# The first projection of a decoder trunk, fed by single k-tiles instead of four-tile blocks

## The chip, the cores and the metric

The kernel runs on one core of a Trainium2 chip. The metric is the device time of one execution in microseconds (us). Before the change the median of three runs was 577.66 us, the lowest 577.63, the highest 577.92.

The engines carry short names. PE is TensorE's matmul, PEld its weight load, DVE is VectorE, ACT is ScalarE, POOL is GpSimd, and SP is SyncE, which here only issues DMAs.

## The reference

One layer on 256 tokens of width 2048, all float32:

```
h    = rmsnorm(x) * g                     # row scale r = rsqrt(mean(x^2) + eps)
proj = h @ w_in                           # 2048 x 8192: dq dk dv mq mk mv gate
d_out, m_out = diff_attention(...), moba_attention(...)   # 8 + 8 heads, causal, ALiBi
x    = x + (concat(d_out, m_out) * silu(gate)) @ w_out
x    = x + memory cross-attention (4 heads) over rmsnorm(mem)
out  = rmsnorm(x) * final_g
```

The change touches only the beginning of `h @ w_in` and the mean of x² that goes with it.

## The kernel before

Every float32 product is made of three matmuls on rounded parts: an operand a is split into a_hi (rounded) and a_lo = a − a_hi, and a @ w becomes a_hi @ w_hi + a_hi @ w_lo + a_lo @ w_hi. ACT makes the hi part of every weight slab, DVE the lo part, and PE multiplies.

The projection goes by 8 pairs of heads. A pair needs 16 halves. A half is two k-tiles (2 × 128 rows of w_in) by 512 columns. Halves 0 to 7 of a pair make q and k in PSUM banks 0 and 1, halves 8 to 15 make v and the gate in banks 2 and 3. For a half PE runs 12 matmuls (2 k-tiles × 2 token tiles × 3 products), in `half_group` (L557 to L575).

The weight slabs go round through three buffers: `w_raw` (8 halves deep, filled by SP's DMAs), `w_hi` and `w_lo` (4 halves deep). ACT's `split_hi` (L803) may run as far ahead as the four slots allow, since it waits only for the DMA and for the half that used the slot before. DVE's `split_lo` (L1119) follows it. So the two converters can have up to four halves ready before PE needs them. A semaphore counts each step: `half_loaded`, `hi_made`, `lo_made`, `half_done`.

The left operand of the first pair is x itself, not yet scaled by r. It has to be turned so that the model dimension lies on the partitions. PE does this with transposes against an identity matrix, in `transpose_block` (L583): a block is four k-tiles, 8 transposes, into two PSUM banks. ACT (`block_hi_bank`, L822) then multiplies by the gain and rounds to `aT_hi`, DVE (`block_lo_bank`, L1138) makes `aT_lo`. Block 0 is turned before the first matmul, and blocks 1, 2 and 3 after halves 0, 2 and 4. x comes in five DMAs. While PE has nothing to do at the start it multiplies the identity by itself (`keep_busy`, 5, 4 and 2 times).

Between the halves the engines do other things, at places that the program fixes by the number n of the half. ACT squares and sums all of x at n = 4 and n = 5 (L1019). DVE, at n = 6, right after the lo part of half 8, copies the other gains and works out r = 1/sqrt(mean) by an integer seed and Newton steps, a chain of small dependent instructions (L1322 to L1332). Only then comes the lo part of half 9. The queues are in order on every engine: an instruction that waits holds all that stand behind it.

After the 16 halves of pair 0 the other seven pairs and the later stages follow in the same way, all fed by the same three buffers. The change leaves them as they are.

Of the kernel before, what the change touches and what calls it, by code (L numbers as in the profile page):

```python
# [22 lines left out]
F32 = mybir.dt.float32  # L23
# [7 lines left out]
P = 128  # L31
# [49 lines left out]
BLOCKS = (("x", 0, 4), ("x", 1, 6), ("x", 2, 4), ("x", 3, 6))  # L81


# [11 lines left out]
X_PARTS = ((0, 256), (256, 512), (512, 1024), (1024, 1536), (1536, 2048))  # L95
WARM_UP = (5, 4, 2)
# [31 lines left out]
def program(nc, x, mem, norm_mix_g, w_in, lambda_q1, lambda_k1, lambda_q2, lambda_k2,  # L128
            subln_g, w_out, norm_mem_g, mem_norm_g, w_q_mem, w_kv_mem, w_o_mem, final_g, out):
    with ExitStack() as ctx:  # L130
# [102 lines left out]
        x_sq, at = columns(0, NT)  # L233
        x_ms, at = columns(at, NT)
# [52 lines left out]
        first_hi = sem("first_hi")  # L287
        first_lo = sem("first_lo")
# [7 lines left out]
        block_made = sem("block_made")  # L296
        block_hi = sem("block_hi")
        block_lo = sem("block_lo")
# [8 lines left out]
        x_ms_ready = sem("x_ms_ready")  # L307
# [114 lines left out]
        def _(sp):  # L422
# [48 lines left out]
            load_x(0)  # L471
            for n in range(PAIR_HALVES):
                load_pair_half(DIFF, 0, 0, n)
                if n in (0, 1, 3, 5):
                    load_x((n + 1) // 2 + 1)
# [80 lines left out]
        def _(pe):  # L556
            def half_group(half, slot, banks, hi, lo, k0, first, last):  # L557


                first_half = isinstance(half, int) and half == 0  # L560
                if first_half:
                    pe.wait_ge(first_lo, 1)
                else:
                    wait(pe, lo_made, half + 1)
                for k in range(GK // 2):
                    if first_half and k == 1:
                        pe.wait_ge(lo_made, 1)
# [15 lines left out]
            def transpose_block(b):  # L583

                source, n, bank = BLOCKS[b]
                rows_of = {"x": xs, "mem": mems, "x1": xs}[source]
                before = [c for c in range(b) if BLOCKS[c][2] == bank]
                if source == "x" and n > 0:
                    pe.wait_ge(x_loaded[n + 1], 16)
                if source == "mem":  # L590
                    pe.wait_ge(mem_loaded, 16)
                if source == "x1":
                    pe.wait_ge(x1_ready, NT * (n + 1))
                if before:
                    pe.wait_ge(block_lo, 2 * (before[-1] + 1))
                for i in range(2):
                    if source == "x" and n == 0:
                        pe.wait_ge(x_loaded[i], 16)
                    for k in range(2):
                        for t in range(NT):  # L600
                            col = n * COLS + (2 * i + k) * P
                            m = pe.transpose(ps[:, bank + i, (k * NT + t) * P:(k * NT + t + 1) * P],  # L602
                                             rows_of[:, t, col:col + P], ident[:, :])
                    m.then_inc(block_made, 1)
                    if source == "x" and n == 0:
                        keep_busy(WARM_UP[1 + i])
# [42 lines left out]
            def pair_window(j, kind, first=False):  # L649

                for n in range(PAIR_HALVES):
# [7 lines left out]
                    if first and n < PAIR_HALVES // 2:  # L659
                        pe.wait_ge(block_lo, n + 1)  # L660
                    half_group(PAIR_HALVES * j + n, n % SPLITS, (0, 1) if n < PAIR_HALVES // 2 else (2, 3),
                               aT_hi, aT_lo, within * (GK // 2), within == 0, within == 2 * NG - 1)
                    if first:
                        if n in (0, 2, 4):
                            transpose_block(1 + n // 2)
# [17 lines left out]
            transpose_block(0)  # L683
# [120 lines left out]
        def _(act):  # L804
            def split_hi(half, i, turn, tail=False):
# [9 lines left out]
                if isinstance(half, int) and half == 0:  # L815

                    act.activation(w_hi[:, 0, 0], raw[:, 0], ACT.Copy).then_inc(first_hi, 1)
                    act.activation(w_hi[:, 0, 1], raw[:, 1], ACT.Copy).then_inc(hi_made, 1)
                    return
                act.activation(w_hi[:, i % SPLITS], raw, ACT.Copy).then_inc(hi_made, 1)  # L820

            def block_hi_bank(b, i):  # L822

                source, n, bank = BLOCKS[b]
                first_gain = {"x": 0, "x1": KO, "mem": 2 * KO}[source]
                act.wait_ge(block_made, 2 * b + i + 1)
                for k in (2 * i, 2 * i + 1):
                    into = cT_hi[:, k] if source == "x1" else aT_hi[:, GK * n + k]
                    gain = first_gain + GK * n + k
                    m = act.activation(into, ps[:, bank + i, (k % 2) * SEQ:(k % 2 + 1) * SEQ], ACT.Identity,  # L830
                                       scale=gainsT[:, gain:gain + 1])
                m.then_inc(block_hi, 1)
# [170 lines left out]
            block_hi_bank(0, 0)  # L1003
            split_hi(0, 0, 0)
            block_hi_bank(0, 1)
            split_hi(1, 1, 0)
            block_hi_bank(1, 0)
            split_hi(2, 2, 0)
            block_hi_bank(1, 1)
            for n in range(PAIR_HALVES):  # L1010
                if n in (3, 4, 5, 6):
                    block_hi_bank((n + 1) // 2, (n + 1) % 2)
                if n > 0:
                    split_hi(n + 2, n + 2, 0)
                if n == 4:
                    for part_loaded in x_loaded:
                        act.wait_ge(part_loaded, 16)
                if n in (4, 5):
                    act.activation(junk_row, xs[:, n - 4, :], ACT.Square,  # L1019
                                   accum_out=x_sq[:, n - 4:n - 3]).then_inc(x_summed, 1)  # L1020
                    act.wait_ge(x_summed, n - 3)
# [97 lines left out]
        def _(dve):  # L1119
            def split_lo(half, i, tail=False):  # L1120
# [4 lines left out]
                if isinstance(half, int) and half == 0:  # L1125

                    dve.wait_ge(first_hi, 1)
                    dve.tensor_tensor(lo[:, 0], w_raw[:, 0, 0], hi[:, 0].bitcast(F32), ALU.subtract
                                      ).then_inc(first_lo, 1)
                    dve.wait_ge(hi_made, 1)  # L1130
                    dve.tensor_tensor(lo[:, 1], w_raw[:, 0, 1], hi[:, 1].bitcast(F32), ALU.subtract
                                      ).then_inc(lo_made, 1)
                    return
# [3 lines left out]
            def block_lo_bank(b, i):  # L1137
                source, n, bank = BLOCKS[b]  # L1138
                first_gain = {"x": 0, "x1": KO, "mem": 2 * KO}[source]
                dve.wait_ge(block_hi, 2 * b + i + 1)  # L1140
                for k in (2 * i, 2 * i + 1):
# [365 lines left out]
```

## Time and profile before

| | before |
|---|---|
| median of three runs | 577.66 us |
| the profiled execution | 577.68 us |
| its span, first to last instruction | 575.9 us |
| PE busy | 565.1 us, 98% of the span |
| DVE, ACT busy | 422.8 us, 405.3 us |
| mean granted TensorE clock | 0.995 of full speed |
| first matmul of the projection | 8.33 us after the span's start |
| first matmul of half 8 | 33.61 us |

The span leaves out 1.78 us of the profiled execution that lie around it. The busy share of PE counts a matmul from its start to its modelled end, and neighbours overlap, so the distance between the starts of two matmuls is the better measure of the pace.

### The profile page before, as it was taken

To read this page: it belongs to the slowest core of one execution; us is meant where nothing else is said; L and a number is where in the kernel's file an instruction comes from. 1 tells how busy PE (TensorE), PEld (TensorE's weight loads), DVE (VectorE), ACT (ScalarE), POOL (GpSimd) and SP (SyncE) were. 2 spreads that over 40 slices of the span, in tenths; PEclk is the share of its full clock that TensorE was granted. 3 is DMA by queue.
4 is the path that set the end of the run, shared out by engine and by line. 5 is a ranking of instruction groups with operands and counts; after the bars stand their busy time and mean duration, and the time that the engine had idled before them with its cause. 6 is when DMAs were issued, how large, how long until landed. Compare 5 with 4: busy or idle time off the path is not lost.

```text
span 575.9 us, 8620 instructions
## 1 busy us (share of the span) xinstructions
PE 565.1 (98%) x2666; PEld 471.2 (82%) x2666; DVE 422.8 (73%) x710; ACT 405.3 (70%) x643; POOL 1.9 (0%) x25
## 2 busy tenths in 40 slices
PE   8999999999999999999999999999999999999993
PEld 7788888888888888888888888888888888888883
DVE  4678769778886877866766767767577887865875
ACT  5776967967868768766775784784589786845623
POOL 1000000000000000000000000000000000000000
PEclk9999999999999999999999999999999999999998
DMA  8997769658676776885875974979699977984203
GB/s 277 328 277 254 212 164 254 183 187 232 189 232 195 196 223 188 220 244 160 247 223 143 277 197 158 236 207 318 206 248 277 249 227 220 237 225 142 103 1 146
DMA packets 147356, 122.40 MB, mean 213 GB/s; under 512 B 63057, under 2 KB 129154, under 8 KB 146818
## 3 DMA queue, kind: packets, MB, share of 16 engines
q1 hardware_dynamic: 147298, 122.08, 73.4%
q8 instruction: 12, 0.20, 0.1%
q14 instruction: 14, 0.11, 0.1%
q10 hardware_dynamic: 32, 0.01, 0.0%
HBM read 106.06 MB, written 2.10 MB: 188 GB/s over the span
## 4 chain that ended last, share of the span: by engine, by line
PE 97%; DMA 1%; DVE 0%; SPq 0%; ACT 0%; issue 0%; ACTq 0%; DVEq 0%
PE ps L571 29%; PE ps L572 29%; PE ps L573 29%; PE ps L638 2%; PE ps L789 1%; PE ps L785 1%; PE ps L784 1%; PE ps L620 1%; DMA xs<-in_x 1%; PE ps L758 1%; PE ps L738 1%; PE ps L602 1%; PE ps L623 0%; PE ps L747 0%; PE ps L626 0%; SPq L432 0%
## 5 line engine op out<-in xcount | busy, mean ns | idle before, releaser
L1135 DVE TENSOR_TENSOR w_lo<-w_raw,w_hi 128x1024 fp32r<-128x1024 f32 x187 | 227.6, 1223 | 109.0 <-ACT w_hi L820 106.6
L820 ACT ACTIVATE w_hi<-w_raw 128x1024 fp32r<-128x1024 f32 x187 | 197.0, 1057 | 86.6 <-PE ps L573 84.6
L571 PE MATMUL ps<-w_hi,aT 128*128 128x512 f32 x576 | 226.5, 393 | 0.1
L572 PE MATMUL ps<-w_lo,aT 128*128 128x512 f32 x576 | 224.3, 389 | 0.0
L573 PE MATMUL ps<-w_hi,aT 128*128 128x512 f32 x576 | 224.2, 389 | 0.0
L573 PEld LDWEIGHTS ps<-w_hi,aT 128*128 128x128 f32 x576 | 108.1, 188 | 22.8
L571 PEld LDWEIGHTS ps<-w_hi,aT 128*128 128x128 f32 x576 | 108.2, 188 | 22.6 <-issue 0.5
L572 PEld LDWEIGHTS ps<-w_lo,aT 128*128 128x128 f32 x576 | 108.2, 188 | 21.6
L571 PE MATMUL ps<-w_hi,yT_hi 128*128 128x512 f32 x144 | 56.2, 390 | 0.0
L573 PE MATMUL ps<-w_hi,yT_lo 128*128 128x512 f32 x144 | 56.0, 389 | 0.0
L572 PE MATMUL ps<-w_lo,yT_hi 128*128 128x512 f32 x144 | 56.0, 389 | 0.0
L573 PEld LDWEIGHTS ps<-w_hi,yT_lo 128*128 128x128 f32 x144 | 27.0, 188 | 5.7
L571 PEld LDWEIGHTS ps<-w_hi,yT_hi 128*128 128x128 f32 x144 | 27.0, 188 | 5.6
L572 PEld LDWEIGHTS ps<-w_lo,yT_hi 128*128 128x128 f32 x144 | 27.0, 188 | 5.5
L1191 DVE RECIPROCAL pool<-pool 128x128 f32<-128x128 f32 x32 | 30.5, 953 | 1.1
L920 ACT ACTIVATE mems<-ps 128x1024 uint16<-128x1024 uint16 x16 | 15.5, 1020 | 18.5 <-PE ps L573 18.5
L941 ACT ACTIVATE pool<-pool,small 128x256 f32<-128x256 f32 (+1 forms) x48 | 21.3, 444 | 7.1 <-DVE small L1226 7.1
L890 ACT ACTIVATE pool<-mems 128x1024 uint16<-128x1024 uint16 x16 | 21.8, 1362 | 2.5 <-DMA mems<-mems 2.5
L1218 DVE SCALAR_TENSOR_TENSOR pool<-ps,small,alibi 128x256 f32<-128x256 f32 (+2 forms) x32 | 15.0, 512 | 5.8 <-PE ps L626 5.8
L1106 ACT ACTIVATE pool<-xs 128x512 f32<-128x512 f32 (+1 forms) x9 | 5.3, 586 | 15.3 <-DVE xs L1451 15.3
L881 ACT ACTIVATE probT<-mems 128x768 uint16<-128x768 uint16 x16 | 16.0, 1079 | 0.0
L955 ACT ACTIVATE mems<-pool 128x768 uint16<-128x768 uint16 x16 | 13.3, 832 | 2.9 <-DVE pool L1243 2.9
(181 smaller groups left out, 507.1 us busy)
## 6 DMA issues: line engine op xcount, KB each, us to landing
w_raw<-in_w_in SPq DMA_DIRECT2D x256, 256.0 KB, 3.2
w_raw<-in_w_out SPq DMA_DIRECT2D x64, 256.0 KB, 3.9
w_raw<-in_w_kv_mem SPq DMA_DIRECT2D x32, 256.0 KB, 4.2
w_raw<-in_w_q_mem SPq DMA_DIRECT2D x16, 256.0 KB, 2.9
w_raw<-in_w_o_mem SPq DMA_DIRECT2D x16, 256.0 KB, 3.4
mems<-in_mem SPq DMA_DIRECT2D x1, 2048.0 KB, 10.2
xs<-in_x SPq DMA_DIRECT2D x3, 512.0 KB, 7.6
w_raw<-in_final_g SPq DMA_DIRECT2D x1, 1024.0 KB, 4.6
```

Source lines behind the costliest of these rows:

```text
L571: pe.matmul(acc, hi[:, k0 + k, tok], w_hi[:, slot, k], start=first and k == 0, stop=False)
L572: pe.matmul(acc, hi[:, k0 + k, tok], w_lo[:, slot, k], start=False, stop=False)
L573: m = pe.matmul(acc, lo[:, k0 + k, tok], w_hi[:, slot, k], start=False, stop=last and k == GK // 2 - 1)
L820: act.activation(w_hi[:, i % SPLITS], raw, ACT.Copy).then_inc(hi_made, 1)
L881: act.activation(probT[:, u].rearrange("p i q -> p (i q)").bitcast(U16) .rearrange("p (c h) -> p h c", h=2), probT_planes[:, u].rearrange( ...
L890: act.activation(qkT_sb[:, :, t * P:(t + 1) * P].bitcast(U16) .rearrange("p i (q h) -> p h i q", h=2), qkT_planes[:, t].rearrange("p (h i ...
L920: act.activation(qk_planes[:, t].rearrange("p (h c) -> p h c", h=2), ps[:, t, :].bitcast(U16).rearrange("p (c h) -> p h c", h=2), ACT.Copy ...
L941: m = act.activation(prob_sb[:, u, c, cols], prob_sb[:, u, c, cols], ACT.Exp, bias=neg_max[:, u, t, c:c + 1], accum_out=exp_sum[:, c, u, t ...
L955: act.activation(prob_planes[:, u].rearrange("p (h c) -> p h c", h=2), prob_sb[:, u, 0, :].bitcast(U16).rearrange("p (c h) -> p h c", h=2) ...
L1135: dve.tensor_tensor(lo, w_raw[:, i % RAW], hi.bitcast(F32), ALU.subtract).then_inc(lo_made, 1)
L1191: dve.reciprocal(s, s).then_inc(silu_steps, 1)
L1218: dve.scalar_tensor_tensor(prob_sb[:, u, 0:kind.maps, cols], banks[:, :, cols], r[:, t:t + 1], bias, ALU.mult, ALU.add).then_inc(logits_re ...
```

## The change

In the first eight halves of pair 0 everything now goes by single k-tiles.

- **Transposes.** `transpose_rows(k)` turns one k-tile (2 transposes) into bank 4 + k mod 4. K-tiles 0 and 1 are turned before the first matmul, and k-tile k + 2 right after the matmuls of k-tile k.
- **Matmuls.** `first_half_group` runs one k-tile at a time: 2 matmuls hi × hi, then a wait for the lo parts, then 4 matmuls. The number of matmuls is the same.
- **ACT and DVE.** They make `aT` and `w` of one k-tile after the other: 128×256 of aT, then 128×512 of w, 16 times. Halves 8 and 9 are converted after k-tile 15, as before in the program's order, but now nothing of them can be done before.
- **Sums of squares.** ACT sums x in four pieces of 128×1024, one at the end of each of its halves 4 to 7. DVE adds the pieces up with one more instruction at the head of the chain for r.
- **Loads.** x comes in seven DMAs instead of five. Each of the first eight halves comes in three DMAs instead of two: one for its first k-tile, two for its second.
- **Warm-up.** The identity products are 3 and 4 instead of 5, 4 and 2.

The diff, cut to its core:

```diff
-BLOCKS = (("x", 0, 4), ("x", 1, 6), ("x", 2, 4), ("x", 3, 6))
...
-X_PARTS = ((0, 256), (256, 512), (512, 1024), (1024, 1536), (1536, 2048))
-WARM_UP = (5, 4, 2)
+X_PARTS = ((0, 128), (128, 256), (256, 512), (512, 768), (768, 1024), (1024, 1536), (1536, 2048))
+X_PART_BEFORE = (0, 2, 3, 4, 5, None, 6, None)
+X_PART_OF = (0, 1, 2, 2, 3, 3, 4, 4, 5, 5, 5, 5, 6, 6, 6, 6)
+WARM_UP = (3, 4)
...
+            def load_first_half(n):
+
+                if X_PART_BEFORE[n] is not None:
+                    load_x(X_PART_BEFORE[n])
+                sp.dma_start(w_raw[:, n, 0, :].rearrange("p (s c) -> p s c", c=2 * P),
+                             in_slabs[n][:, 0, 0:2, 0:2 * P]).then_inc(k_loaded[n], 16)
+                if n == 0:
+                    load_x(1)
+                for part, slab in enumerate(SLABS["diff", 0]):
+                    sp.dma_start(w_raw[:, n, 1, part * 2 * P:(part + 1) * 2 * P], in_slabs[n][:, 1, slab, 0:2 * P]
+                                 ).then_inc(half_loaded[n], 16)
...
+            def transpose_rows(k):
+
+                pe.wait_ge(x_loaded[X_PART_OF[k]], 16)
+                wait(pe, rows_lo, k - 3)
+                for t in range(NT):
+                    m = pe.transpose(ps[:, 4 + k % 4, t * P:(t + 1) * P], xs[:, t, k * P:(k + 1) * P], ident[:, :])
+                m.then_inc(rows_made, 1)
+
+            def first_half_group(n):
...
+                for i in range(GK // 2):
+                    k = 2 * n + i
+                    first, last = k == 0, k == KO - 1
+                    pe.wait_ge(rows_hi, k + 1)
+                    pe.wait_ge((k_hi, hi_made)[i], n + 1)
+                    for t in range(NT):
+                        pe.matmul(ps[:, t, :], aT_hi[:, k, t * P:(t + 1) * P], w_hi[:, slot, i],
+                                  start=first, stop=False)
+                    pe.wait_ge(rows_lo, k + 1)
+                    pe.wait_ge((k_lo, lo_made)[i], n + 1)
+                    for t in range(NT):
+                        pe.matmul(ps[:, t, :], aT_hi[:, k, t * P:(t + 1) * P], w_lo[:, slot, i],
+                                  start=False, stop=False)
+                        m = pe.matmul(ps[:, t, :], aT_lo[:, k, t * P:(t + 1) * P], w_hi[:, slot, i],
+                                      start=False, stop=last)
+                    if i == 1:
+                        m.then_inc(half_done, 1)
+                    if k + 2 < KO:
+                        transpose_rows(k + 2)
...
             pe.transpose(ps[:, 3, 0:KO], mix_gain[:, :], ident[0:KO, 0:KO]).then_inc(gainsT_made, 1)
-            transpose_block(0)
+            transpose_rows(0)
+            keep_busy(WARM_UP[1])
+            transpose_rows(1)
...
+            def first_split_hi(n):
+
+                for i in range(GK // 2):
+                    k = 2 * n + i
+                    act.wait_ge(rows_made, k + 1)
+                    act.activation(aT_hi[:, k], ps[:, 4 + k % 4, 0:SEQ], ACT.Identity, scale=gainsT[:, k:k + 1]
+                                   ).then_inc(rows_hi, 1)
...
+                    act.activation(w_hi[:, n % SPLITS, i], w_raw[:, n, i], ACT.Copy).then_inc((k_hi, hi_made)[i], 1)
...
+            for n in range(2 * NG):
+                first_split_hi(n)
+                if n >= 4:
+                    sum_squares(n % 2, (n - 4) // 2)
+            for n in range(2 * NG - 2, PAIR_HALVES):
+                split_hi(n + 2, n + 2, 0)
...
+            def first_split_lo(n):
+
+                for i in range(GK // 2):
+                    k = 2 * n + i
+                    dve.wait_ge(rows_hi, k + 1)
+                    dve.scalar_tensor_tensor(aT_lo[:, k], ps[:, 4 + k % 4, 0:SEQ], gainsT[:, k:k + 1],
+                                             aT_hi[:, k].bitcast(F32), ALU.mult, ALU.subtract).then_inc(rows_lo, 1)
+                    dve.wait_ge((k_hi, hi_made)[i], n + 1)
+                    dve.tensor_tensor(w_lo[:, n % SPLITS, i], w_raw[:, n, i], w_hi[:, n % SPLITS, i].bitcast(F32),
+                                      ALU.subtract).then_inc((k_lo, lo_made)[i], 1)
...
+                    dve.tensor_reduce(x_sq, x_sq2, axis=AX.X, op=ALU.add).then_inc(x_total, 1)
```

PE, the end of the start-up and the first half, in the kernel before. L602 are transposes of x, L571 to L573 the three products:

```order
L602 MATMUL ps<-ident,xs 128x128 x4
L580 UNCONDITIONAL_BRANCH
L581 MATMUL ps<-ident 128x128
L580 REGISTER_ALU
L580 COMPARE_AND_BRANCH
L571 MATMUL ps<-w_hi,aT 128x512
L572 MATMUL ps<-w_lo,aT 128x512
L573 MATMUL ps<-w_hi,aT 128x512
```

PE at the same place in the changed kernel. L595 are the transposes of x, L608 is hi × hi, L613 and L615 are the two products with a lo part:

```order
L595 MATMUL ps<-ident,xs 128x128 x2
L608 MATMUL ps<-w_hi,aT 128x512 x2
L613 MATMUL ps<-w_lo,aT 128x512
L615 MATMUL ps<-w_hi,aT 128x512
L613 MATMUL ps<-w_lo,aT 128x512
L615 MATMUL ps<-w_hi,aT 128x512
L595 MATMUL ps<-ident,xs 128x128 x2
L608 MATMUL ps<-w_hi,aT 128x512 x2
```

A pair of transposes now stands behind every six matmuls, 14 times, where a block of eight stood three times.

ACT from the w_hi of half 6 to that of half 9, in the kernel before (L820 makes w_hi, L830 makes aT_hi, L1019 sums squares):

```order
L820 ACTIVATE w_hi<-w_raw 128x1024
L1019 ACTIVATE pool,small<-xs 128x2048
L830 ACTIVATE aT<-ps,gainsT 128x256 x2
L820 ACTIVATE w_hi<-w_raw 128x1024
L1019 ACTIVATE pool,small<-xs 128x2048
L830 ACTIVATE aT<-ps,gainsT 128x256 x2
L820 ACTIVATE w_hi<-w_raw 128x1024 x3
```

ACT in the changed kernel, from k-tile 12 (half 6) to the halves 8 to 10. L837 makes aT_hi, L844 makes w_hi of one k-tile, L1021 sums squares, L830 makes w_hi of a whole half:

```order
L837 ACTIVATE aT<-ps,gainsT 128x256
L844 ACTIVATE w_hi<-w_raw 128x512
L837 ACTIVATE aT<-ps,gainsT 128x256
L844 ACTIVATE w_hi<-w_raw 128x512
L1021 ACTIVATE pool,small<-xs 128x1024
L837 ACTIVATE aT<-ps,gainsT 128x256
L844 ACTIVATE w_hi<-w_raw 128x512
L837 ACTIVATE aT<-ps,gainsT 128x256
L844 ACTIVATE w_hi<-w_raw 128x512
L1021 ACTIVATE pool,small<-xs 128x1024
L830 ACTIVATE w_hi<-w_raw 128x1024 x3
```

Before, the w_hi of half 8 is the second of the last three; after, it is the first, and the last aT_hi and a sum of squares stand right in front of it.

## Rows read from the trace of the kernel before

**Rows 1.** The page: busy time by engine, and the chain that ended last.

```profile
PE 565.1 (98%) x2666; PEld 471.2 (82%) x2666; DVE 422.8 (73%) x710; ACT 405.3 (70%) x643; POOL 1.9 (0%) x25
PE 97%; DMA 1%; DVE 0%; SPq 0%; ACT 0%; issue 0%; ACTq 0%; DVEq 0%
```

**Rows 2.** Timeline of PE, start-up: start, duration, engine, line, operation, idle time before.

```profile
1.73 2.51 PE L581 MATMUL ps<-ident 128*128 128x128 f32 x10 [1.73 <-POOL ident L542]
...
4.39 1.11 PE L602 MATMUL ps<-ident,xs 128*128 128x128 f32 x4
5.30 1.91 PE L581 MATMUL ps<-ident 128*128 128x128 f32 x8
7.46 0.66 PE L602 MATMUL ps<-ident,xs 128*128 128x128 f32 x4 [0.24 <-DMA xs<-in_x]
...
8.33 0.47 PE L571 MATMUL ps<-w_hi,aT 128*128 128x512 f32 x1
```

**Rows 3.** Timeline of PE after half 9: a pair of transposes between matmuls.

```profile
38.82 0.39 PE L573 MATMUL ps<-w_hi,aT 128*128 128x512 f32 x1
39.05 0.38 PE L673 MATMUL ps<-ident,pool 128*128 128x128 f32 x2
39.19 0.48 PE L571 MATMUL ps<-w_hi,aT 128*128 128x512 f32 x1
39.50 0.39 PE L572 MATMUL ps<-w_lo,aT 128*128 128x512 f32 x1
```

**Rows 4.** Timeline of PE: a block of eight transposes, and the step to half 2.

```profile
10.91 0.39 PE L573 MATMUL ps<-w_hi,aT 128*128 128x512 f32 x1
11.14 1.03 PE L602 MATMUL ps<-ident,xs 128*128 128x128 f32 x8
...
12.25 0.40 PE L572 MATMUL ps<-w_lo,aT 128*128 128x512 f32 x1
...
14.52 0.39 PE L573 MATMUL ps<-w_hi,aT 128*128 128x512 f32 x1
14.97 0.47 PE L571 MATMUL ps<-w_hi,aT 128*128 128x512 f32 x1
```

**Rows 5.** Timeline of PE: the last matmul of half 6, the first of halves 7 and 8.

```profile
30.66 0.39 PE L573 MATMUL ps<-w_hi,aT 128*128 128x512 f32 x1
30.89 0.39 PE L571 MATMUL ps<-w_hi,aT 128*128 128x512 f32 x1
...
33.61 0.39 PE L571 MATMUL ps<-w_hi,aT 128*128 128x512 f32 x1
```

**Rows 6.** Timeline of ACT.

```profile
6.76 0.63 ACT L817 ACTIVATE w_hi<-w_raw 128x512 fp32r<-128x512 f32 x1 [0.32 <-DMA w_raw<-in_w_in]
7.30 0.61 ACT L818 ACTIVATE w_hi<-w_raw 128x512 fp32r<-128x512 f32 x1
...
11.78 0.84 ACT L830 ACTIVATE aT<-ps,gainsT 128x256 fp32r<-128x256 f32 x2 [1.83 <-PE ps L602]
12.51 1.06 ACT L820 ACTIVATE w_hi<-w_raw 128x1024 fp32r<-128x1024 f32 x1
...
21.77 1.93 ACT L1019 ACTIVATE pool<-xs 128x2048 f32<-128x2048 f32 x1
23.57 0.21 ACT L1019 ACTIVATION_READ_ACCUMULATOR pool<-xs 128x1 f32 x1
```

**Rows 7.** Timeline of DVE.

```profile
7.42 0.69 DVE L1128 TENSOR_TENSOR w_lo<-w_raw,w_hi 128x512 fp32r<-128x512 f32 x1
...
13.60 1.23 DVE L1135 TENSOR_TENSOR w_lo<-w_raw,w_hi 128x1024 fp32r<-128x1024 f32 x1
...
31.52 0.19 DVE L1322 COPY gainsT<-ps 128x33 f32<-128x33 f32 x1
...
34.39 3.56 DVE L1135 TENSOR_TENSOR w_lo<-w_raw,w_hi 128x1024 fp32r<-128x1024 f32 x3
```

**Rows 8.** Busy time by stage, start-up left out; last columns: granted clock, DMA share, GB/s.

```profile
8.30:33.60 25.30, 25.24 (x124) 20.59 (x123) 17.63 (x35) 18.88 (x28) 0.00 (x0) 1.00 1.02 335
```

More of the change, by code:

```diff
@@ L233, in program @@
         x_sq, at = columns(0, NT)
+        x_sq2, at = columns(at, NT, 2)
         x_ms, at = columns(at, NT)
@@ L286, in program @@
         half_loaded = [sem(f"half_loaded{s}") for s in range(RAW)]
-        first_hi = sem("first_hi")
-        first_lo = sem("first_lo")
+        k_loaded = [sem(f"k_loaded{n}") for n in range(2 * NG)]
+        k_hi = sem("k_hi")
+        k_lo = sem("k_lo")
         hi_made = sem("hi_made")
@@ L306, in program @@
         x_summed = sem("x_summed")
-        x_ms_ready = sem("x_ms_ready")
+        x_total = sem("x_total")
         r_x_steps = sem("r_x_steps")
@@ L557, in half_group @@
             def half_group(half, slot, banks, hi, lo, k0, first, last):
[L560 to L564, printed above, removed]
+                wait(pe, lo_made, half + 1)
                 for k in range(GK // 2):
-                    if first_half and k == 1:
-                        pe.wait_ge(lo_made, 1)
                     for t in range(NT):
@@ L581, in keep_busy @@
                     pe.matmul(ps[:, 2, 0:P], ident[:, :], ident[:, :], start=True, stop=True)
[L583 to L606, printed above, removed]
@@ L814, in split_hi @@
                 wait(act, half_done, half - behind + 1)
[L815 to L819, printed above, removed]
                 act.activation(w_hi[:, i % SPLITS], raw, ACT.Copy).then_inc(hi_made, 1)
[L822 to L832, printed above, removed]
+            def first_split_hi(n):
[4 more added lines that the diff above has]
+                                   ).then_inc(rows_hi, 1)
+                    if i == 0:
+                        act.wait_ge(k_loaded[n], 16)
+                        wait(act, half_done, n - SPLITS + 1)
+                    else:
+                        act.wait_ge(half_loaded[n], 32)
+                    act.activation(w_hi[:, n % SPLITS, i], w_raw[:, n, i], ACT.Copy).then_inc((k_hi, hi_made)[i], 1)
             def split_turn(b, t):
@@ L1002, in _, with sum_squares @@
             act.wait_ge(gainsT_ready, 1)
[L1003 to L1021, printed above, removed]
+            def sum_squares(t, part):
+                loaded = range(5) if part == 0 else range(5, len(X_PARTS))
+                for n in loaded:
+                    act.wait_ge(x_loaded[n], 16)
+                cols = slice(part * DM // 2, (part + 1) * DM // 2)
+                act.activation(junk_row[:, 0:DM // 2], xs[:, t, cols], ACT.Square,
+                               accum_out=x_sq2[:, t, part:part + 1]).then_inc(x_summed, 1)
+                act.wait_ge(x_summed, 2 * part + t + 1)
+            for n in range(2 * NG):
[4 more added lines that the diff above has]
+                split_hi(n + 2, n + 2, 0)
                 if n == 10:
@@ L1124, in split_lo @@
                 lo = wo_lo[:, i - WO_HALF0] if over_yT else w_lo[:, i % SPLITS]
[L1125 to L1133, printed above, removed]
                 dve.wait_ge(hi_made, half + 1)
                 dve.tensor_tensor(lo, w_raw[:, i % RAW], hi.bitcast(F32), ALU.subtract).then_inc(lo_made, 1)
[L1137 to L1141, printed above, removed]
-                    hi, lo = (cT_hi[:, k], cT_lo[:, k]) if source == "x1" else \
-                             (aT_hi[:, GK * n + k], aT_lo[:, GK * n + k])
-                    gain = first_gain + GK * n + k
-                    m = dve.scalar_tensor_tensor(lo, ps[:, bank + i, (k % 2) * SEQ:(k % 2 + 1) * SEQ],
-                                                 gainsT[:, gain:gain + 1], hi.bitcast(F32),
-                                                 ALU.mult, ALU.subtract)
-                m.then_inc(block_lo, 1)
+            def first_split_lo(n):
[7 more added lines that the diff above has]
+                                      ALU.subtract).then_inc((k_lo, lo_made)[i], 1)
             def merge_turn(b):
@@ L1307, in _ @@
             dve.wait_ge(gainsT_ready, 1)
[L1308 to L1319 removed]
+            for n in range(2 * NG):
+                first_split_lo(n)
+            for n in range(2 * NG - 2, PAIR_HALVES):
+                split_lo(n + 2, n + 2)
                 if n == 6:
```

39 lines of the change are left out of this document (14 added, 25 removed).

## The prediction, made before the changed kernel was run

> **What bounds the kernel now.** I read the page first. PE is busy for 98% of the span and the chain that ended last is PE for 97% [rows 1]: the kernel is one long stream of matmuls, and no other engine holds it for long. The stages, in the view by windows, say the same for the stretch that the change touches. From 8.30 to 33.60 us PE is busy for 25.24 of 25.30 us at the full granted clock, while ACT and DVE are busy for 18.88 and 17.63 us [rows 8]. So a microsecond saved or lost in PE's stream before half 9 should stand unchanged in the end time, and I only have to find by how much the stream moves at that point. I take half 9 as the mark because what lies behind it is the same in both kernels. In the kernel before, half 8 starts at 33.61 [rows 5], and half 9 12 matmuls later. The pace is 2.72 us per half (30.89 to 33.61, rows 5), or 0.227 us per matmul. That puts half 9 at 36.33.
>
> Then I read the timelines of PE, ACT and DVE up to 40 us, since the change is about who is ahead of whom.
>
> **The start.** Now PE turns four tiles at 4.39, spins on the identity from 5.30, turns four more at 7.46 when the second part of x has landed, and starts the projection at 8.33 [rows 2]. The early operations are slow: eight identity records take 1.91 us, some 0.21 us from one to the next, and the transposes from 4.39 to 5.30 are 0.23 us apart. After the change two transposes instead of four stand at 4.39, so the identity products begin 0.46 us earlier, at 4.84; eight records of 0.21 end their slots at 6.55; two transposes follow, and the first matmul can start at about 7.05. Is its data there? ACT's first aT_hi can start at 5.15 (two transposes, the last ending near 5.08, and the 0.07 us from a transpose's end to ACT worked out below) and w_hi of k-tile 0 at 5.52, to end at 6.15. Its DMA is the second in the queue, 384 KB behind the start. In the kernel before 256 KB had landed by 4.39 [rows 2] and 768 KB by 6.76, where ACT waited for it [rows 6]; in proportion 384 KB land near 5.0. w_lo of k-tile 0 takes 0.69 us on DVE [rows 7] and ends near 6.9. So the first matmul stands at 7.05, **1.28 us earlier**. The bounds: 6.3 if the early operations run at the later pace, 7.5 if x's second part again comes when it came before. I take 7.05, from the rows at the pace that this stretch shows. The shorter first warm-up (3 for 5) falls into the wait for the gains' DMA, so I cost it at nothing. It could cost something only through the clock, a rival below.
>
> **PE's own stream.** The matmuls are the same 96. A block of eight transposes costs, from 10.91 to 12.25, 1.34 us less two paces of 0.227, that is 0.886 [rows 4]. The trace also has a lone pair of transposes, at 39.05: from 38.82 to 39.50 are 0.68 us less 0.454, so 0.226 [rows 3]. Three blocks (2.66) go and 14 pairs (3.16) come: **+0.50**. The bounds for a pair are 0.20 (a quarter of a block is 0.22) and 0.33, if the slow first matmul behind a pair were not shared as it is here. The 0.22 us that PE loses before half 2 (14.52 to 14.97, less 0.227, rows 4), where it waits for DVE's lo part that ends at 14.83 [rows 7], goes too: **−0.22**. If PE waited for nothing, half 8 would start at 33.61 − 1.28 + 0.50 − 0.22 = 32.61 and the kernel would gain 1.0 us.
>
> Waits come far more often: 48 instructions of PE's now carry one in this stretch, some 36 more than before. The step into half 7, which waits for two semaphores long met, takes 30.66 to 30.89, the plain pace [rows 5]: a wait already met costs nothing, and I cost them so. The Trainium skill (Advanced Engine Details and Errata, Miscellaneous Facts) gives 50 to 100 ns for reading a semaphore's value from a sequencer. If each of the 36 waits cost that in PE's stream, it would be an estimated 1.8 to 3.6 us more. The trace disagrees for a wait of this kind.
>
> **Where PE will wait.** K-tile k + 2 is turned after the matmuls of k, so ACT and DVE have the matmuls of k + 1 (1.59 us with its pair) to make both of its operands, and can never be further ahead. From the start of k-tile k: six matmuls 1.36; second transpose 0.10 later, 0.27 long; and ACT starts 0.07 after it (in the block at 11.14 the fourth transpose ends near 11.71 and ACT starts at 11.78, rows 4, 6). That is 1.80. One aT_hi takes ACT 0.365 to the next instruction (11.78 to 12.51 for two), w_hi of a k-tile 0.54 (6.76 to 7.30) and ends after 0.62 [rows 6]; w_lo begins 0.03 later and takes 0.69 [rows 7]; PE needs 0.14 more (14.83 to 14.97). The lo parts are ready at 1.80 + 0.365 + 0.62 + 0.03 + 0.69 + 0.14 = 3.64. PE wants them at 2 × 1.587 + 0.454 = 3.63. It just fits, with no reserve; I charge nothing.
>
> Four times ACT has a sum of squares behind its second k-tile. The trace only has the whole row: 1.80 us to the next instruction and 0.21 for the read [rows 6]. Half of it I take as 0.95 + 0.23 = **1.18** (w_hi of the same 1024 columns shows 0.95 from one to the next); the bounds are 1.0 and the whole 2.0. After the sum in half 4 ACT starts aT_hi of k-tile 10 at 0.905 + 1.18 = 2.09 after that of k-tile 9, and 1.59 would be in time: PE waits **0.50**. That delay is then slack for the next sum, and the gains' transpose after half 5 is slack for the third; I put 0.15 there.
>
> Now halves 8 and 9. In the kernel before DVE's chain for r starts at 31.52 and the lo part of half 9 at 34.39 [rows 7], so half 8 was ready at 31.6, two microseconds early, and half 9 at 34.39 + 1.23 = 35.62, 0.7 early. That lead is what the change takes away. After it:
> - half 8 without further waits at 32.61 + 0.50 = 33.11; k-tile 13 starts 4.31 before (1.587 + 2 × 1.36), at 28.80, and aT_hi of k-tile 15 at 28.80 + 1.80 = 30.60
> - ACT: + 0.905 (aT_hi, w_hi) + 1.18 (last sum) + 1.06 (w_hi of half 8) = 33.74
> - DVE: lo part of half 8, 33.77 + 1.23 = 35.00. PE should have started half 8 at 33.26 and stands for some 2.2 us, till the gain that follows the lo part is written too
> - DVE goes on at 34.91 with its chain, 34.39 − 31.52 = 2.87 us, then the lo part of half 9, 37.78 + 1.23 = 39.01; PE starts half 9 at 39.15, after another wait of 1.0
>
> Half 9 moves from 36.33 to 39.15: **+2.82 us**. The one more instruction in the chain (0.16 or so) is within the rounding. Behind this DVE converts a half in 1.2 us against PE's 2.72, so the lead comes back and PE waits no more; the transposes of q and k that SP sends off behind the lo part of half 9 move with it. Added to the profiled execution's own 577.68 us, which stands 0.02 above the median, this gives **580.5 us**.
>
> **Rivals.**
> A. *PE's clock rises later.* Rows 2 show slow transposes at 4.39 and quick ones at 7.46 (0.66 for four). If the shorter warm-up lets the rise slip behind the first matmuls, these run at twice the distance, 0.227 us more for each. Eight of them cost 1.8 us: 582.3. Against it: PE has nothing to do from about 3.3 to 4.17 only.
> B. *The loads come late.* SP issues ten DMAs more, about 0.5 us each; k-tile 14 would be sent off near 21 instead of 16 us. ACT wants it at 29. The queue moves 335 GB/s with its share at 1.02 [rows 8], and 6.1 MB need 18 us of that. If the smaller pieces cost a quarter of that rate, the last halves land some 1.3 us late: 581.8. The Trainium skill (DMA: Bandwidth & Descriptors, Anatomy of one DMA) gives each DMA about 2 us fixed, and half efficiency at some 860 KB. Pieces of 256 KB one behind the other would then reach an estimated 100 GB/s; the trace shows 335, so the fixed part overlaps here.
> C. *No stop at halves 8 and 9*, the not-slower side. If ACT and DVE are ahead after all, PE's stream alone decides and the end comes 1.0 us earlier: 576.7, within what can't be told from no change. For that the lo part of half 9 must be ready by 35.3, 3.7 us sooner than worked out. For it speaks that ACT and DVE have a quarter of this stretch free [rows 8]; against it that this free time lies before the transposes on which they wait.
> D. *As C, with the start at the early bound*: 0.75 less, 575.9, faster.
>
> **The numbers.** 0.2% of this kernel is 1.16 us, about what a measurement of it can tell from no change. My forecast holds with 0.64, with its own range 579.3 to 581.7: −1.2 for a sum or chain partly hidden and the start at its early bound, +1.2 for dearer pairs and a dearer sum. A has 0.10, B 0.07, C 0.12, D 0.05; 0.02 is for PE waits that cost by themselves. The range, 577.8 to 582.7, leaves out C and D and the ends of A. Faster by over 0.2% has 0.05, within 0.2% has 0.13, slower has 0.82.
>
> **What would show it.** In the changed kernel's profile: the first matmul near 7.05; k-tiles 1.59 us apart, with short waits for DVE's w_lo; a wait of half a microsecond at k-tile 10; PE idle for about 2 us before half 8 on DVE and for 1 us before half 9; and no idle time that was not there before after that. I am wrong if half 9 starts before 38 us, if PE waits at the k-tiles all along, or if the first matmuls are 0.4 us apart.

## The result

| | before | after |
|---|---|---|
| median | 577.80 us (5 runs, 577.63 to 578.33) | 580.67 us (5 runs, 580.43 to 580.96) |
| ratio, 95% interval | | 1.0049 [1.0038, 1.0060] |
| span of the profiled execution | 575.9 us | 578.6 us |
| first matmul of the projection | 8.33 us | 6.02 us |
| first matmul of half 8, of half 9 | 33.61, 36.33 us | 35.03, 38.93 us |

The changed kernel is 2.9 us slower. The forecast was 580.5, with the range 577.8 to 582.7. In later visits to the chip one execution of the kernel before (of 31) and one of `e4_three_ahead` (of 10) took some 1480 us; why is not known, and the intervals leave both out.

Here are PE's waits in the profile of the changed kernel (engine, line, whom it waited for: us in total, times, longest):

```profile
PE ps L588 <- POOL ident L555: 1.7, 1, 1.7
PE ps L578 <- DVE small L1314: 1.7, 1, 1.7
PE ps L578 <- DVE w_lo L1135: 0.9, 1, 0.9
```

The first was there before. The other two are new and stand before half 8 and half 9. L1314 is the small gain that DVE writes right behind the lo part of half 8, and PE waits for it too before it starts that half. The timeline of PE around them:

```profile
32.94 0.40 PE L615 MATMUL ps<-w_hi,aT 128*128 128x512 f32 x1
35.03 0.49 PE L578 MATMUL ps<-w_hi,aT 128*128 128x512 f32 x1 [1.69 <-DVE small L1314]
...
37.67 0.39 PE L580 MATMUL ps<-w_hi,aT 128*128 128x512 f32 x1
38.93 0.50 PE L578 MATMUL ps<-w_hi,aT 128*128 128x512 f32 x1 [0.87 <-DVE w_lo L1135]
```

At the plain pace of 0.227 us half 8 would start at 33.17 and half 9 2.72 us after half 8, at 37.75. So PE loses 1.86 and 1.18 us; the idle time in brackets is shorter, since it counts from the modelled end of the matmul before. ACT and DVE show what PE waits for:

```profile
30.31 0.47 ACT L837 ACTIVATE aT<-ps,gainsT 128x256 fp32r<-128x256 f32 x1 [0.53 <-PE ps L595]
30.68 0.62 ACT L844 ACTIVATE w_hi<-w_raw 128x512 fp32r<-128x512 f32 x1
31.20 1.05 ACT L1021 ACTIVATE pool<-xs 128x1024 f32<-128x1024 f32 x1
32.15 0.19 ACT L1021 ACTIVATION_READ_ACCUMULATOR pool<-xs 128x1 f32 x1
32.37 2.95 ACT L830 ACTIVATE w_hi<-w_raw 128x1024 fp32r<-128x1024 f32 x3
```

```profile
33.46 1.23 DVE L1135 TENSOR_TENSOR w_lo<-w_raw,w_hi 128x1024 fp32r<-128x1024 f32 x1 [1.44 <-ACT w_hi L830]
34.60 0.18 DVE L1312 COPY gainsT<-ps 128x33 f32<-128x33 f32 x1
...
37.66 3.49 DVE L1135 TENSOR_TENSOR w_lo<-w_raw,w_hi 128x1024 fp32r<-128x1024 f32 x3
```

The chain for r started at 31.52 before and the lo part of half 9 at 34.39 [rows 7]; they start at 34.60 and 37.66 now. From the start of half 9 to the end of the span it is 539.6 us before and 539.7 after: in the profiles all of the difference, 2.6 to 2.7 us, arises ahead of half 9. (The profiled execution of the changed kernel, 580.43 us, is the fastest of its five; the medians are 2.9 apart.)

### The profile page after: what moved, and what is told of

Read it like the earlier page. It is cut to its first block, busy times and chain, and to the rows that moved or that the text cites. A ratio compares the mean times of both kernels' runs of the same rounds, so it can differ in the third digit from the quotient of the medians.

```text
span 578.6 us, 8663 instructions
## 1 busy us (share of the span) xinstructions
PE 565.6 (98%) x2658; PEld 468.9 (81%) x2658; DVE 425.0 (73%) x718; ACT 407.0 (70%) x654; POOL 1.9 (0%) x25
## 4 chain that ended last, share of the span: by engine, by line
PE 97%; DVE 1%; ACT 1%; issue 0%; POOL 0%; ACTq 0%; POOLq 0%; DVEq 0%
PE ps L578 28%; PE ps L579 27%; PE ps L580 27%; PE ps L652 2%; PE ps L799 1%; PE ps L804 1%; PE ps L800 1%; PE ps L608 1%; PE ps L613 1%; PE ps L634 1%; PE ps L615 1%; PE ps L595 1%; PE ps L773 1%; PE ps L753 1%; PE ps L588 1%; DVE w_lo L1135 0%
## 5 line engine op out<-in xcount | busy, mean ns | idle before, releaser
L1135 DVE TENSOR_TENSOR w_lo<-w_raw,w_hi 128x1024 fp32r<-128x1024 f32 x180 | 218.9, 1222 | 107.6 <-ACT w_hi L830 105.7
L830 ACT ACTIVATE w_hi<-w_raw 128x1024 fp32r<-128x1024 f32 x180 | 189.5, 1057 | 84.7 <-PE ps L580 83.7
L578 PE MATMUL ps<-w_hi,aT 128*128 128x512 f32 x544 | 213.7, 393 | 2.6 <-DVE small L1314 1.7
L579 PE MATMUL ps<-w_lo,aT 128*128 128x512 f32 x544 | 211.9, 390 | 0.0
L580 PE MATMUL ps<-w_hi,aT 128*128 128x512 f32 x544 | 211.7, 389 | 0.0
L578 PEld LDWEIGHTS ps<-w_hi,aT 128*128 128x128 f32 x544 | 102.1, 188 | 24.4 <-DVE small L1314 2.1
L580 PEld LDWEIGHTS ps<-w_hi,aT 128*128 128x128 f32 x544 | 102.1, 188 | 21.4
L579 PEld LDWEIGHTS ps<-w_lo,aT 128*128 128x128 f32 x544 | 102.2, 188 | 20.5
```

Source lines behind the costliest of these rows:

```text
L1135: dve.tensor_tensor(lo, w_raw[:, i % RAW], hi.bitcast(F32), ALU.subtract).then_inc(lo_made, 1)
```

## The experiments

All times are medians. "Before" is the kernel before on the same chip, 577.6 to 577.8 us. The differences between the changed kernel and an experiment are taken across chip visits; where half 9 in the profile is the finer measure I give it too.

**What set the start of the kernel before.** `e1_warm_before`:

```diff
-WARM_UP = (5, 4, 2)
+WARM_UP = (3, 4, 2)
```

> The kernel before with the first warm-up cut from 5 to 3 identity products, nothing else. The changed kernel began its first transposes at 3.54 us instead of 4.39. Theory (loads): the start of the kernel before is set by the second part of x, which lands near 7.4 us; the first transposes move to about 3.5, the second four stay at 7.4 to 7.5, the first matmul stays at 8.3, half 9 at 36.3 and the time at 577.8, give or take 0.3. Rival (warm-up): the start is set by PE's warm-up; first matmul near 7.5, half 9 near 35.5, time 577.0.

577.80 us, ratio 0.9997 [0.9988, 1.0007]. The timeline of PE in its profile:

```profile
3.77 1.12 PE L602 MATMUL ps<-ident,xs 128*128 128x128 f32 x4 [0.17 <-DMA xs<-in_x]
4.68 1.92 PE L581 MATMUL ps<-ident 128*128 128x128 f32 x8
7.51 0.66 PE L602 MATMUL ps<-ident,xs 128*128 128x128 f32 x4 [0.91 <-DMA xs<-in_x]
...
8.37 0.47 PE L571 MATMUL ps<-w_hi,aT 128*128 128x512 f32 x1
```

The first transposes come 0.6 us earlier and PE then idles for 0.91 us for x. The loads set the start before, as the theory had it: by itself the shorter warm-up gives nothing. The changed kernel has no such wait, and its second transposes start at 5.73. Both parts of its start count there. With the five products put back (next run) its first matmul comes at 6.87, so the single k-tiles and the smaller pieces of x are worth 1.5 of the 2.3 us, and the shorter warm-up, once they are there, the other 0.85.

**What the early start is worth.** `e5_warm_after` puts the 5 back into the changed kernel:

```diff
-WARM_UP = (3, 4)
+WARM_UP = (5, 4)
```

> The changed kernel with the first warm-up back at 5 identity products instead of 3. In its profile the first matmul stands at 6.02 us, but the first two take 0.46 us from one to the next, twice the later pace, and k-tile 1 starts at 8.0 to 8.4. Theory (the slow matmuls at the start give back most of the earlier start): the first matmul comes at 6.8 to 6.9 and nearly all run at the full pace, k-tile 1 at 8.4 to 8.6, half 9 0.2 to 0.5 us later than 38.9, time 580.9. Rival (every microsecond of PE's start counts in full): half 9 at 39.8, time 581.5.

580.93 us, 1.0053 [1.0037, 1.0068]. First matmul at 6.87, k-tile 1 at 8.88, half 9 at 39.84. In this profile the first two matmuls are slow as well (1.10 us for the two, as in the changed kernel), so half 9 moves by the whole 0.9 us, as the rival said. The median moves by only 0.3 against 580.67, taken on another visit, and its interval holds both. The theory that the slow matmuls eat the earlier start is not borne out by the trace and not refuted by the time; I leave it open.

**The order of DVE.** `e2_chain_behind_half9` moves the chain for r behind the lo part of half 9:

```diff
-                if n == 6:
+                if n == 7:
                     dve.wait_ge(x_summed, 2 * NT)
```

> The changed kernel with DVE's chain for r moved one half later, behind the lo part of half 9; the copy of the other gains stays where it was. Theory (lost lead, two stops): the stop before half 8 stays (half 8 at 35.0), the stop of 1.2 us before half 9 goes (half 9 at 37.8), and the time falls by 1.1 to 579.5. Rival (the stops are something else than DVE's order, such as the transposes of q and k or the slots): half 9 stays at 38.9 and the time at 580.6, or the stop moves behind half 9.

579.37 us, 1.0026 [1.0016, 1.0036], 1.3 less than the changed kernel. PE's only new wait in the profile stands before half 8:

```profile
35.48 0.50 PE L578 MATMUL ps<-w_hi,aT 128*128 128x512 f32 x1 [1.69 <-DVE small L1314]
```

Half 9 follows without a gap, at 38.34. That is 0.6 earlier than in the changed kernel and not the 1.1 expected, because k-tile 1 starts 0.45 later here, at 8.46. So the second stop is DVE's chain, and nothing takes its place.

**The sums.** `e3_no_sums` leaves them out (DVE writes a constant in their place):

```diff
-                act.activation(junk_row[:, 0:DM // 2], xs[:, t, cols], ACT.Square,
-                               accum_out=x_sq2[:, t, part:part + 1]).then_inc(x_summed, 1)
-                act.wait_ge(x_summed, 2 * part + t + 1)
...
+            dve.memset(x_sq2, DM / 2.0).then_inc(x_summed, 1)
```

> The changed kernel without ACT's four sums of squares; DVE writes 1024 into each piece instead, so r is that of a mean square of 1 and the sum of squares is left out of the computation. Theory (the sums hold ACT): k-tile 10 starts 0.2 to 0.4 us earlier, the lo part of half 8 comes 1.2 + 0.4 us earlier, half 8 starts near 33.4 instead of 35.0, half 9 near 37.2 instead of 38.9, time 579.0. Rival (ACT's own work without the sums already takes all the time that it has): half 8 starts at 34.5 or later.

578.92 us, 1.0020 [1.0010, 1.0029], 1.75 less. In its profile half 8 starts at 33.98 behind an idle 0.51 us, in spite of a first k-tile 0.4 us slower. From k-tile 1 to half 8 it is 25.6 us instead of 27.0. The first stop is thus for the greater part ACT's sums. A rest of 0.7 us (33.98 less 33.07 + 0.23) stays without any sum; that it is what a lead of two k-tiles costs here is worked out by this difference, and the run with three k-tiles bears on it below. The second stop is still there, 0.91 us of idle time, and half 9 starts at 37.89, not near 37.2.

**The same work, better placed.** `e6_sums_in_pieces` keeps the sums, in eight pieces behind k-tiles 4 to 11:

```diff
+                    if 4 <= k < 12:
+                        sum_squares(i, n - 2)
...
-                if n >= 4:
-                    sum_squares(n % 2, (n - 4) // 2)
```

> The changed kernel with the sums of squares in eight pieces of 128x512 behind the k-tiles 4 to 11, in ACT's idle time of about 0.65 us each, instead of four of 128x1024 behind k-tiles 9, 11, 13 and 15. A piece should take about 0.75 us. Theory (the last sum stands in front of half 8): half 8 starts as in the run without sums, 25.6 us after k-tile 1 instead of 27.0, so near 33.7, and half 9 near 37.6; time 579.3. Rival (the pieces don't fit, each delays its k-tile by 0.1 us and more): k-tiles 4 to 12 come 1.75 us apart and half 8 is no earlier than 34.7; time 580.3.

579.52 us, 1.0031 [1.0019, 1.0043]. Half 8 at 33.62, half 9 at 37.52, 25.7 us from k-tile 1 to half 8. That is as expected. A piece takes 0.78 us of ACT, and the k-tiles come 1.66 apart: with aT_hi (0.37) and w_hi (0.52) the piece fills ACT's time for a k-tile, so the pieces fit with nothing to spare. The median is 0.6 above that of `e3_no_sums`, though the profile is earlier by 0.4 at half 9: its profiled execution had a quick start (below) and is the fastest of its six.

**The lead.** `e4_three_ahead` turns k + 3 instead of k + 2:

```diff
-                    if k + 2 < KO:
-                        transpose_rows(k + 2)
+                    if k == 0:
+                        transpose_rows(2)
+                    if k + 3 < KO:
+                        transpose_rows(k + 3)
```

> The changed kernel with the transposes three k-tiles ahead instead of two, from k-tile 3 on; nothing else. Theory (the two-tile lead is what costs): the k-tiles come 1.59 us apart instead of 1.645, k-tile 10 does not wait, and the last transposes come one k-tile earlier, so that the lo part of half 8 comes 1.6 to 2.5 us earlier. Half 8 starts near 32.8, half 9 near 36.7, time 578.4. Rival (ACT and DVE are at their rate, and a longer lead gives nothing): k-tiles stay 1.64 apart, half 8 near 35.0, time 580.6.

578.66 us, 1.0014 [1.0004, 1.0024], 2.0 less. The k-tiles come 1.61 us apart against 1.64, k-tile 10 does not wait, half 8 starts at 32.98 and half 9 at 36.89, each 2.0 us earlier. (From k-tile 1 to half 8 it is 24.7 us against 27.0, but 0.2 of that is the pair for k-tile 3, which now stands ahead of k-tile 1.) Both stops are still there, smaller and equal:

```profile
PE ps L578 <- DVE w_lo L1137: 0.9, 1, 0.9
PE ps L578 <- DVE small L1316: 0.7, 1, 0.7
```

One k-tile more of lead, on the same ACT and DVE, gives 2.0 of the 2.9 us back. ACT and DVE are not at their rate; they were kept waiting for transposes.

**All three together.** `e7_all_three` is the sum of the last edits (chain, pieces, three ahead):

> The changed kernel with all three repairs: transposes three k-tiles ahead, sums in eight pieces behind k-tiles 4 to 11, DVE's chain for r behind the lo part of half 9. Theory (all that was lost was the lead): no stop before half 8 or half 9; half 8 near 32.3, half 9 near 35.0, 1.3 us ahead of the kernel before, time 576.4. Rival (another wait takes their place: half 10's lo part behind the chain, or the transposes of q and k): half 9 near 35.0 but a stop between half 10 and the scores, time 577.5 or more.

577.91 us, 1.0001 [0.9992, 1.0010]: no stop before half 8 or 9, but 1.5 us less gained than expected. Half 9 starts at 35.89, not near 35.0. Two other waits have come:

```profile
10.68 0.44 PE L595 MATMUL ps<-ident,xs 128*128 128x128 f32 x2 [0.85 <-DMA xs<-in_x]
...
50.35 0.50 PE L636 MATMUL ps<-kT_parts,qT_hi 64*128 64x256 f32 x4 [0.45 <-DVE kT_parts L1205]
```

The first is a part of x that lands late. In `e4_three_ahead`, with the same order of loads, PE took this part at 9.72 and did not wait, so its landing differs between executions. The second is the turned k, which comes from a DMA transpose that SP sends off behind a queue of loads. So in this profile the loads had become the bound. The windows from 16 to 24 us (last columns: granted clock, DMA share, GB/s) show a hole in the loads, which is much smaller in the kernel before. First that kernel:

```profile
16.00:24.00 8.00, 8.00 (x41) 6.69 (x40) 5.99 (x8) 6.42 (x9) 0.00 (x0) 1.00 0.94 307
```

then in `e7_all_three`:

```profile
16.00:24.00 8.00, 8.00 (x41) 6.49 (x40) 5.70 (x11) 7.84 (x20) 0.00 (x0) 1.00 0.66 208
```

The hole lies from 20 to 24 us (89 and 101 GB/s by 2 us); the kernel before has a dip to 194 GB/s from 20 to 22 alone. SP spends 0.40 to 0.47 us on most of these DMAs, from 32 KB (lambda) to 512 KB (a part of x). With ten more of them the first load of half 8 is sent off at 19.81 us instead of 16.99. The four small ones for lambda stand in front of half 7 in both kernels. In the changed kernel the hole is there too (208 GB/s), but PE does not feel it. The same rows show the other reserve used up: ACT, with the pieces, is busy for 7.84 of the 8 us.

**The second warm-up.** `e8_short_second_warm` is `e7_all_three` with:

```diff
-WARM_UP = (3, 4)
+WARM_UP = (3, 2)
```

> The run before with the second warm-up at 2 identity products instead of 4. Theory (data allow it, and the slow level lasts until the same moment): the second transposes start near 5.1 instead of 5.7 if x's second part has landed, the first matmul near 5.5, one more matmul runs slow, and k-tile 1 starts 0.1 to 0.3 us earlier; time 0.2 us lower, 576.2. Rival (PE's clock rises later with less work before): k-tile 1 starts later than 8.4, and the time is 0.5 us or more above the run before.

577.93 us, 1.0000 [0.9991, 1.0009], the same as without. The first matmul comes at 5.63, but all six of k-tile 0 are slow, 0.43 us apart:

```profile
5.63 1.20 PE L608 MATMUL ps<-w_hi,aT 128*128 128x512 f32 x2
6.63 0.63 PE L613 MATMUL ps<-w_lo,aT 128*128 128x512 f32 x1
7.06 0.63 PE L615 MATMUL ps<-w_hi,aT 128*128 128x512 f32 x1
```

K-tile 1 starts at 9.04, and half 9 at 36.08. The trace looks like the rival, the time does not: it is not 0.5 us above the run before. That it is the shorter warm-up and not chance is not shown, since nearly the same happens in the next run with the warm-up unchanged.

**The loads.** `e10_loads_only` changes the loads of the changed kernel, and nothing else. The table of the parts of x, which puts the part with k-tiles 4 and 5 ahead of the weights of k-tile 3, and ACT's wait that goes with it are left out here:

```diff
-                if n < 2 * NG:
-                    load_first_half(n)
+                if n < 3:
+                    load_first_half(n)
+                elif n < 2 * NG:
+                    if X_PART_BEFORE[n] is not None:
+                        load_x(X_PART_BEFORE[n])
+                    load_pair_half(DIFF, 0, 0, n)
...
-                if n == 6:
+                if n == 10:
                     for i, vec in enumerate((lambda_q1, lambda_k1, lambda_q2, lambda_k2)):
```

> The changed kernel with the changed order of loads alone, without the three repairs. Theory (in the changed kernel ACT and DVE, not the loads, are late before halves 8 and 9): half 8 stays at 35.0 and half 9 at 38.9, give or take 0.4 for the slow matmuls at the start, time 580.6. Rival (the loads hold ACT or DVE, and that is part of the loss): half 9 a microsecond earlier, time 579.6.

581.07 us, 1.0057 [1.0042, 1.0072]. The hole is gone (353 GB/s from 16 to 24 us) and the stops stay at 1.70 and 0.89 us of idle time. Half 9 starts at 39.66, 0.7 later than in the changed kernel, and k-tile 1 by the same 0.7: a slow first k-tile. From k-tile 1 to half 9 it is 31.0 us against 30.9. The loads play no part in what the change lost. The run moves the lambda loads and merges others at once, so it does not say which of the two filled the hole.

`e9_repairs_and_loads` has both, `e7_all_three` and these loads:

> The kernel with all three repairs and a changed order of loads: the part of x with k-tiles 4 and 5 comes before the weights of k-tile 3, the halves 3 to 7 come in two DMAs again instead of three, and the four small loads for lambda stand behind half 10 instead of half 6. With the repairs alone PE waited 0.85 us for x at k-tile 4 and 0.45 us for the turned k at the scores, and the DMAs moved 208 GB/s from 16 to 24 us against 307 in the kernel before. Theory (the loads took over as the bound): no wait for x at k-tile 4, k-tile 4 starts near 11.4 and half 9 near 34.9 instead of 35.9, DMAs at 300 GB/s or more from 16 to 24, no wait at the scores, time 576.5. Rival (the waits come from something else, or the time is lost again behind the scores): half 9 moves but the time stays within 0.3 of 577.9.

576.93 us against 577.63, **0.9988 [0.9979, 0.9997]**: the one version that beats both kernels, by 0.7 us. 352 GB/s from 16 to 24 us, no wait at k-tile 4 nor at the scores. Half 9 starts at 35.58, 0.3 earlier than with the repairs alone and not near the 34.9 expected; the wait at the scores that has gone was 0.45. The interval of this run and that of `e7_all_three` still meet at their ends. The profile has one wait for the loads left, now where PE turns k-tiles 2 and 3:

```profile
8.56 0.66 PE L601 MATMUL ps<-ident,xs 128*128 128x128 f32 x4 [1.19 <-DMA xs<-in_x]
```

`e11_smaller_x` goes after that one. It splits this part of x in two (its loads are left out here) and lets PE turn the tiles one by one at first:

```diff
-                    if k == 0:
-                        transpose_rows(2)
-                    if k + 3 < KO:
+                    if k < 2:
+                        transpose_rows(k + 2)
+                    if 0 < k < KO - 3:
```

> The run before (repairs and loads) with the part of x for k-tiles 2 and 3 split in two; PE turns k-tile 2 behind k-tile 0, k-tiles 3 and 4 behind k-tile 1, then three ahead as before. In the profile of the run before PE waited 1.19 us at 8.56 us for that part of x. Theory (this part's landing is what is left of the loads): no wait behind k-tile 0, k-tile 1 near 7.9 to 8.4, half 9 0.5 to 1.0 us earlier than 35.6, time 576.3. Rival (the small parts only move the wait to k-tile 3 or 4): time 576.9.

577.03 us, 0.9992 [0.9983, 1.0001]: no better. K-tile 1 starts at 7.33, 1.6 us earlier than in the run before, and yet half 9 is 0.2 later, at 35.79. The lead is lost mostly at ACT, which waits for weights:

```profile
12.12 0.63 ACT L853 ACTIVATE w_hi<-w_raw 128x512 fp32r<-128x512 f32 x1 [1.03 <-DMA w_raw<-in_w_in]
...
16.08 0.63 ACT L853 ACTIVATE w_hi<-w_raw 128x512 fp32r<-128x512 f32 x1 [0.57 <-DMA w_raw<-in_w_in]
```

The rival was right: small parts move the wait. In these two profiles, with the conversions out of the way, the first 16 us are bound by how fast x and the weights arrive.

## Why the prediction was right

**The stops at halves 8 and 9: right in mechanism and size.** Half 9 was put at 39.15 and is at 38.93, a shift of 2.60 instead of 2.82. The pieces of that sum:

| | predicted | trace |
|---|---|---|
| half 8, if nothing held it | 33.26 | 33.17 |
| lo part of half 8 ready | 35.00 | 34.69 |
| stop before half 8 | some 2.2 | 1.86 |
| chain for r (the trace has one more instruction) | 2.87 | 3.06 |
| lo part of half 9 ready | 39.01 | 38.9 |
| stop before half 9 | 1.0 | 1.18 |
| a sum of 1024 columns | 1.18 | 1.17 |
| a pair of transposes | 0.226 | 0.24 |

The runs show both causes apart: the chain's place is worth 1.3 us, the sums 1.75, the third k-tile of lead 2.0. They overlap: the sums and the lead both act on the first stop.

**The start: the wrong size, and a wrong reading.** The first matmul came at 6.02, not 7.05. "The shorter first warm-up (3 for 5) falls into the wait for the gains' DMA, so I cost it at nothing" was the error. Rows 2 end the ten identity records at 4.24 and the gains' transpose follows at 4.17: PE was the late one, and the gains had landed by 3.33. With six records everything behind them moves by 0.85 us, as long as x is there; `e1_warm_before` shows that before it was not. The remaining 0.2 lie in the spacing at the start.

**The k-tiles: the mechanism seen, the reserve misread.** "It just fits, with no reserve; I charge nothing." From k-tile 1 to 9 they come 1.643 us apart, not 1.587, which is 0.45 us in all. PE does wait, on every second one, for w_lo. The row of DVE is the w_lo of k-tile 4, ready at 13.29. PE begins with it at 13.47, as soon behind it as at other waits for DVE, and the next matmul comes 0.28 later, against 0.24 a k-tile on:

```profile
12.60 0.69 DVE L1145 TENSOR_TENSOR w_lo<-w_raw,w_hi 128x512 fp32r<-128x512 f32 x1
...
13.47 0.44 PE L613 MATMUL ps<-w_lo,aT 128*128 128x512 f32 x1
13.75 0.40 PE L615 MATMUL ps<-w_hi,aT 128*128 128x512 f32 x1
...
15.13 0.40 PE L613 MATMUL ps<-w_lo,aT 128*128 128x512 f32 x1
15.37 0.39 PE L615 MATMUL ps<-w_hi,aT 128*128 128x512 f32 x1
```

The wait closes a loop: w_lo releases four matmuls, the transposes of the tile after next follow, then ACT and DVE. That round takes 0.97 to the transposes, 0.42 to ACT's start, 1.72 to the end of w_lo and 0.17 to PE, 3.28 us for two k-tiles, against 3.17 for PE alone. The prediction's own terms give 3.19 for the round, so a reserve of nothing was a shortage of 0.02 at best; the measured round is 0.09 longer, 0.06 of it in the four matmuls. The first k-tile, with two slow matmuls, took 0.40 more. These 0.85 us and the early start's 1.03 nearly cancel. From k-tile 9 to 11 it is 3.68 us, 0.51 more than two plain k-tiles, against the 0.50 put down for k-tile 10.

So the sum came out within 0.3 us in part by luck: it put the start 1.03 too late, and two terms worth 0.85 us at nothing. Two of the signs that the prediction gave for being wrong did show, if small. PE waits at every second k-tile, and the first two matmuls are some 0.46 apart. The third sign, half 9 before 38 us, did not show: both stops are there, near their forecast sizes.

**The rivals.** A, the slow pace at the start, came in part: two matmuls of the changed kernel run at it, and more in other runs. That the shorter warm-up is the reason is not shown: with five products again (`e5_warm_after`) the first two are slow as well. B, late loads, did not touch the changed kernel, as `e10_loads_only` shows; in the profiles it became true once the stops were gone. SP sent half 7 off at 18.30 us, not near 21. The section of the Trainium skill that B cites (DMA: Bandwidth & Descriptors, Anatomy of one DMA) gives its 2 us for DMAs that GpSimd issues, and these are SP's; nothing of the sum hung on it. C and D fail on the two waits. That waits already met cost PE nothing holds: the 1.59 us from k-tile 13 to 14 are the 1.587 of the plain pace, with three waits in them. The Trainium skill (Advanced Engine Details and Errata, Miscellaneous Facts) gives 50 to 100 ns for reading a semaphore's value from a sequencer; if each of the three waits cost that, it would be an estimated 0.15 to 0.3 us more. The measurement decides against that here.

## What to carry to other kernels

When work on one engine is handed to others in smaller portions, ask how far ahead they may run, not only whether each portion fits. Here the finer start won 2.3 us at the first matmul and lost 4.9 up to half 9. Of these, 3.0 went at the two stops where the helpers had a long job, since a lead of two tiles could not carry a 1.2 us sum or a 3 us chain. Jobs without a hurry belong in pieces into the helpers' idle time, or behind the portion that is awaited.

## What the runs showed of the hardware

The slow pace at the start ends at a moment that differs from run to run, with the same instructions ahead of it. In the first 8 us the PE programs of the changed kernel, of `e6_sums_in_pieces` and of `e10_loads_only` are the same up to the first matmuls. In the first the pace quickens near 6.9 us. In the second the identity records from 4.02 take 1.56 us instead of 1.91, and all matmuls are quick:

```profile
4.02 1.56 PE L588 MATMUL ps<-ident 128*128 128x128 f32 x8
5.42 0.38 PE L595 MATMUL ps<-ident,xs 128*128 128x128 f32 x2
5.56 0.71 PE L608 MATMUL ps<-w_hi,aT 128*128 128x512 f32 x2
```

In the third the matmuls are 0.43 us apart until 8.3, against the later 0.23:

```profile
7.02 0.63 PE L619 MATMUL ps<-w_lo,aT 128*128 128x512 f32 x1
7.45 0.63 PE L621 MATMUL ps<-w_hi,aT 128*128 128x512 f32 x1
```

Five more profiles have the same start: the pace quickens near 6.9 us in `e4_three_ahead` and `e7_all_three`, near 7.8 in `e2_chain_behind_half9` and `e3_no_sums`, and before 5.6 in `e9_repairs_and_loads`. Up to there PE is busy almost without a break from 1.73 us on in all of them.

The ratio, 1.9, is near the factor of two between the two levels of TensorE's clock, 1.2 and 2.4 GHz, and I take it for that. The column of the granted clock does not confirm it: it reads 1.00 in every window before 9 us of these profiles.

A kernel that starts its real matmuls inside this stretch may inherit the spread. `e9_repairs_and_loads` has runs from 576.0 to 577.6, while the kernel before, whose first matmul at 8.33 is quick, has 577.5 to 578.2 on the same visit. That the pace makes this spread is not shown: x lands at different moments as well, only one execution of each run has a trace, and the five runs of the changed kernel lie within 0.5 us.
